# First layer: gate products strip by strip; third layer: q and k copies inside the softplus

## What is computed

```python
# first layer
o_attn = swa_sink_attention(q, k, v, sinks[i])      # 8 heads, softmax with a sink
...
y = jnp.einsum('blgn,gpn->blgp', h_re, c_re) - jnp.einsum('blgn,gpn->blgp', h_im, c_im)
y = y.reshape(b, l, SSM_WIDTH) + d_skip.astype(f32) * uf
y = jax.nn.gelu(y)
out = y * jax.nn.sigmoid(y @ w_glu.astype(f32) + b_glu.astype(f32))
...
mixed = jnp.concatenate([o_attn, o_ssm], axis=-1) @ even_w_out[i]

# stick-breaking attention, 16 heads
z = jnp.einsum('bhqd,bhkd->bhqk', q_blk, kt).astype(jnp.float32) * scale
log_keep = jnp.where(mask, jax.nn.log_sigmoid(-z), 0.0)
log_survive = lax.cumsum(log_keep, axis=3, reverse=True) - log_keep
weights = jnp.where(mask, jnp.exp(jax.nn.log_sigmoid(z) + log_survive), 0.0)
return jnp.einsum('bhqk,bhkd->bhqd', weights.astype(vt.dtype), vt)
```

## Time and profile before

| | us |
|---|---|
| median of 3 runs | 1596.52 |
| lowest, highest | 1591.95, 1599.69 |
| the profiled execution | 1599.0 |
| its span, first to last instruction | 1597.2 |
| PE busy | 1547.9 (97%) |
| DVE, ACT, POOL busy | 1193.1, 863.6, 262.8 |
| mean granted clock of PE | 0.988 of 2.4 GHz |

### The profile page before, as it was taken

How to read it: one execution, slowest core, us unless ns; L and a number is a source line. 1 busy time by engine, 2 the same in 40 slices (tenths; PEclk the granted TensorE clock), 3 DMA queues, 4 the chain that set the end, 5 groups by cost and what they waited for, 6 DMA issues and landing times.

```text
span 1597.2 us, 30962 instructions
## 1 busy us (share of the span) xinstructions
PE 1547.9 (97%) x10555; PEld 1365.1 (85%) x10555; DVE 1193.1 (75%) x2322; ACT 863.6 (54%) x1323; POOL 262.8 (16%) x110
## 2 busy tenths in 40 slices
PE   7889999999999999999999999999999999999998
PEld 7877888888878887898899999988888888878887
DVE  6987888725778887666599853399999999975555
ACT  6755444458754444746456566555554444445543
POOL 2001000155110001100377856600000000000000
PEclk9899999999999999999999999999999999999999
DMA  6125665543466565433545556555555555555564
GB/s 217 62 80 161 195 192 187 184 146 106 137 195 196 186 194 182 130 100 106 172 159 172 171 177 192 185 171 170 171 171 169 172 171 173 174 178 189 192 196 145
DMA packets 72557, 264.67 MB, mean 166 GB/s; under 512 B 8080, under 2 KB 8336, under 8 KB 72112
## 3 DMA queue, kind: packets, MB, share of 16 engines
q1 hardware_dynamic: 71744, 261.00, 50.6%
q10 hardware_dynamic: 752, 2.83, 0.5%
HBM read 262.75 MB, written 1.05 MB: 165 GB/s over the span
## 4 chain that ended last, share of the span: by engine, by line
PE 87%; DVE 4%; ACT 2%; issue 1%; ACTq 0%; DVEq 0%
PE ps L550 17%; PE ps L639 11%; PE ps L640 11%; PE ps L651 10%; PE ps L554 9%; PE ps L538 6%; PE ps L542 6%; PE ps L539 6%; PE ps L1086 2%; PE ps L584 1%; PE ps L592 1%; PE ps L586 1%; DVE arena L1690 1%; DVE hT L1728 1%; DVE w_lo L1690 1%
## 5 line engine op out<-in xcount | busy, mean ns | idle before, releaser
L1177 ACT ACTIVATE w_hi<-ring 128x1024 fp32r<-128x1024 f32 x489 | 515.7, 1057 | 334.0 <-PE ps L651 206.3
L1690 DVE TENSOR_TENSOR w_lo<-ring,w_hi 128x1024 fp32r<-128x1024 f32 x388 | 473.0, 1220 | 97.7 <-ACT w_hi L1177 83.6
L2537 POOL TENSOR_TENSOR w_lo<-ring,w_hi 128x1024 fp32r<-128x1024 f32 x101 | 254.1, 2528 | 759.8 <-DVE w_lo L1690 378.8
L550 PE MATMUL ps<-hT,w_hi 128*128 128x512 f32 x1216 | 308.8, 395 | 3.3 <-DVE hT L1728 2.6
L639 PE MATMUL ps<-w_hi,halves_hi 128*128 128x512 f32 x688 | 271.5, 395 | 2.5 <-DVE w_lo L1690 2.0
L640 PE MATMUL ps<-w_hi,halves_lo 128*128 128x512 f32 x688 | 268.7, 391 | 0.0
L550 PEld LDWEIGHTS ps<-hT,w_hi 128*128 128x128 f32 x1216 | 220.7, 189 | 47.5 <-issue 3.0
L538 PE MATMUL ps<-hT,w_hi 128*128 128x256 f32 x984 | 250.5, 291 | 5.7 <-DVE hT L1728 3.9
L539 PE MATMUL ps<-hT,w_hi 128*128 128x256 f32 x984 | 246.5, 287 | 0.0
L538 PEld LDWEIGHTS ps<-hT,w_hi 128*128 128x128 f32 x984 | 192.3, 195 | 10.3 <-issue 7.6
L539 PEld LDWEIGHTS ps<-hT,w_hi 128*128 128x128 f32 x984 | 192.6, 196 | 0.0
(11 more groups left out here) (301 smaller groups left out, 1590.5 us busy)
## 6 DMA issues: line engine op xcount, KB each, us to landing
ring<-in_strips SPq DMA_DIRECT2D x489, 512.0 KB, 3.5
const<-in_const SPq DMA_DIRECT2D x1, 1352.0 KB, 11.8
x_s<-in_x SPq DMA_DIRECT2D x2, 512.0 KB, 4.6
arena<-in_rel ACTq DMA_DIRECT2D x1, 1024.0 KB, 5.6
arena<-in_keys ACTq DMA_DIRECT2D x1, 1024.0 KB, 7.2
out<-x_s SPq DMA_DIRECT2D x4, 256.0 KB, 2.3
arena<-in_ssm_bc SPq DMA_DIRECT2D x1, 512.0 KB, 6.9
arena<-in_ssm_b SPq DMA_DIRECT2D x1, 512.0 KB, 8.1
```

Source lines behind the costliest of these rows:

```text
L550: pe.matmul(bank, w[0][:, c * P:(c + 1) * P], hT[:, c].rearrange("p s t -> p (s t)"), start=c == 0, stop=False, skip_group_check=True)
L1177: sc.activation(w_hi[:, n % RING, :], ring[:, n % RING, :], ACT.Copy).then_inc(high_ready, 1)
L1690: return ve.tensor_tensor(o, a, b, op)
L2537: po.tensor_tensor(w_lo[:, n % RING, :], ring[:, n % RING, :], w_hi[:, n % RING, :].bitcast(F32), ALU.subtract).then_inc(low_ready, 1)
```

## The change

Four edits. (1) PE computes all products of gate strip 0, then all of strip 1, and no longer waits for the low half of strip 1 before the first. (2) DVE takes `y(3)` directly behind `y(2)`, ahead of the low half of gate strip 1, and the rest of y(1) behind both; ACT makes the high half of `out` strip 4 ahead of gelu(2) instead of gelu(3). (3) DVE's two `scale_of` calls stand behind the first reduction, and behind the scans of ssm(0). (4) In the third stage the copies of q and k of pairs 1 and 2 are made inside the softplus of the pair before.

```diff
                 def glu(cs):
-                    w = [split(AT[("even", "glu", n)]) for n in range(2)]
-                    low_halves(w[1])
-                    for c in cs:
-                        pe.wait_ge(y_low, c + 1)
-                        for n in range(2):
+                    for n in range(2):
+                        w = split(AT[("even", "glu", n)])
+                        low_halves(w)
+                        for c in cs:
+                            pe.wait_ge(y_low, c + 1)
                             for j in range(2):
...
-                            if c == 3:
-                                mm.then_inc(strip_done, 1)
+                        mm.then_inc(strip_done, 1)
...
                     if j == 2:
-                        high_to(AT[("even", "glu", 1)])
-                    if j == 3:
                         high_to(AT[("even", "out", 4)])
...
-                    if g:
-                        scale_of(0)
                     ve.wait_ge(score_out, 4 * g + 4)
...
                         ch.add(ve.tensor_reduce(two(0)[:, part, :], e_S[g][:, :, lo:hi], AX, ALU.max))
+                        if g and part == 0:
+                            scale_of(0)
...
                     if j == 0:
-                        scale_of(1)
                         ve.wait_ge(decay_rows, 1)
                         ve.wait_ge(zeroed, 5)
                     ch.add(ve.tensor_tensor_scan(z[:, 0, :], m, z[:, 0, :], 0.0, ALU.mult, ALU.add))
                     ch.link(ve.tensor_tensor_scan(z[:, 1, :], m, z[:, 1, :], 0.0, ALU.mult, ALU.add))
+                    if j == 0:
+                        scale_of(1)
...
                 ssm(3)
+                low(AT[("even", "glu", 0)])
                 y(2)
+                y(3)
                 y_rest(1)
-                low(AT[("even", "glu", 0)])
                 low(AT[("even", "glu", 1)])
-                y(3)
                 y_rest(2)
                 y_rest(3)
...
-                def project(j):
+                def project(j, parts=range(2)):
...
                     ve.scalar_tensor_tensor(out=sp, in0=bank_pair(j), scalar=0.0, in1=o_t, op0=ALU.max,
                                             op1=ALU.add).then_inc(sp_ready, 1)
+                    if j < 2:
+                        project(j + 1, [1 - j])
...
                     ve.tensor_copy(o_sp_hi, sp).then_inc(sp_high, 1)
+                    if j == 1:
+                        project(2, [1])
...
                 for j in range(8):
-                    project(j)
+                    if j == 0:
+                        project(0)
+                        project(1, [0])
+                    if j > 2:
+                        project(j)
```

More of the change, by code:

```diff
@@ L766, in glu @@
                 def glu(cs):
-                    w = [split(AT[("even", "glu", n)]) for n in range(2)]
-                    low_halves(w[1])
-                    for c in cs:
-                        pe.wait_ge(y_low, c + 1)
-                        for n in range(2):
+                    for n in range(2):
[3 more added lines that the diff above has]
+                            pe.wait_ge(y_low, c + 1)
                             for j in range(2):
                                 cols = slice(c * T + j * P, c * T + (j + 1) * P)
-                                mm = mm3(ps[:, 6 + n, j * T:(j + 1) * T], w[n][0][:, cols], w[n][1][:, cols],
+                                mm = mm3(ps[:, 6 + n, j * T:(j + 1) * T], w[0][:, cols], w[1][:, cols],
                                          hT_hi[:, c, :], hT_lo[:, c, :], c == 0 and j == 0, c == 3,
                                          skip_group_check=True)
-                            if c == 3:
-                                mm.then_inc(strip_done, 1)
+                        mm.then_inc(strip_done, 1)
                 def probs_turned(ns):
@@ L2094, in diagonal @@
                     return a.rearrange("p h (b c) -> p h b c", c=P)[:, :, 0:3:2, :]
-                def project(j):
+                def project(j, parts=range(2)):
                     if j == 0:
                         ve.wait_ge(evac, FIRST)
-                    for n, (name, dst) in enumerate((("q", o_qT), ("k", o_kT))):
+                    for n in parts:
+                        name, dst = (("q", o_qT), ("k", o_kT))[n]
                         m = FIRST + 2 * j + n
```

## The result

The changed kernel took 1587.73 us (median of four; 1586.53 to 1591.35) against 1597.34 us for the kernel before (median of four, three of them those of the table before): a ratio of 0.9947, 95% interval 0.9921 to 0.9973, 8.5 us less (the two medians are 9.6 us apart). The forecast was 1592.6 us with a range from 1587.5 us: the time lies 0.2 us inside its fast end, and outside the forecast's own range of 1590 to 1596 us. A gain of over 0.5% was given a chance of 0.10.

What follows compares the result with a forecast made beforehand. TensorE, busy 97% of the span, was taken as the bound, so only its waits or lower clock could be won. Gate 2.2 us plus third layer 1.7 us made 3.9 us: 1592.6 us, own range 1590 to 1596, wider range 1587.5 to 1597.5.

Steps and rivals of the forecast that it cites:

- The gate: First layer: gate products strip by strip start `out` strip 4 2.3 us sooner; 2.2 us booked, bounds 1.2 to 2.9.
- the 0.1 us taken off for it: First layer: gate gain of 2.3 us booked as 2.2, since the high half of `out` strip 5 might come late.
- The reciprocals: First layer: first state about 1.2 us sooner, but nothing booked, since later values wait for ACT's normalising.
- The first pair shifts by at most 0.1 us: First layer: moving the first reciprocals behind a DVE reduction, issued about when ACT is done, delays them at most 0.1 us.
- the sum: Whole kernel: 2.2 us at the gate plus 1.7 us in the third layer, 3.9 us, giving 1592.6 us against the median.
- The softplus: Third layer: earlier q and k copies win 3.3 us, less 1.6 us for DVE meeting POOL: 1.7 us, bounds -0.7 to 3.3.
- I take the clock to stay up: Third layer, pair 1: full clock kept behind the new pauses of 0.6 and 1.3 us; 1.5 of 2.7 us won is clock.
- DVE ahead of GpSimd: Rival, third layer: DVE's low part gets in before POOL, or the cost is hidden; gain 5.5 us, 1591.0 us, chance 0.20.
- The clock falls at the new pauses: Rival, gate or pair 1: 3.4 us at the lower clock cost 1.7 us; 1594.3 us, chance 0.13.
- Gate's gain met by the next wait: Rival: `out` strip 5 waits instead, little left in the third layer; 0.5 us in all, 1596 us, chance 0.10.
- GpSimd's meeting in pairs 2 to 7: Rival, third layer: the DVE-POOL meeting recurs, six pairs pay 1.6 us each; 5.7 us slower, 1602.2 us, chance 0.05.

Runs made afterwards that it cites:

- the changed kernel taken again: The kernel with all four edits, run once more without any further edit, against the kernel before: 1587.59 us (6 runs), ratio 0.9948.
- the control: The kernel before, unchanged, run once more as if it were a changed one: 1597.36 us (12 runs), ratio 0.9997.
- the first series: First batch of runs: gate, reciprocals and softplus edits each alone, and all edits again, beside the kernel before (28 runs, mean clock 0.9900).

## Why the prediction was right or wrong

**The gate: right.** Forecast 2.2 us (the times gave 2.3), measured 2.44 to 2.46 us in all nine profiles with the edit. `out` strip 4 starts behind the last gate product with no wait, and strip 5 without one too: its high half was not late, so the 0.1 us taken off for it was not needed. PE had one wait (0.49 us) where two were expected.

**The reciprocals: right that the work gives nothing, wrong that the edit gives nothing.** The 1.3 us sooner at the states (forecast 1.2) and their return at ScalarE's normalising came as told. Two steps were wrong. "The first pair shifts by at most 0.1 us" holds for a late ScalarE only, as in the profile before. Where it comes early, it waits 1.98 us for the reciprocal, and 1.26 us where that stands first, and PE pays those 0.7 us ahead of the first scores. And the sum had no term for the clock: a first state that is earlier divides PE's pause otherwise, and the fall near 80 us, which every profile without the edit has, is missing in seven of eight. The net of the two is small, about 0.4 us by the traces.

**The softplus: right in its chain, by its own steps.** In the changed kernel taken again, z(1) comes 2.6 us sooner on the lead (forecast 2.6), PE waits 1.34 us ahead of cum(0) (1.3), GpSimd starts 0.48 us ahead of DVE's low part (0.4), that part takes 2.69 us (over 2), PE waits 1.45 us (1.6), and the third layer gives 1.85 us (1.7). The Trainium skill ("SBUF — State Buffer", on the two separate sides of SBUF) has the port pair as an exclusive lock for a whole instruction. The run in which GpSimd waits agrees: 0.95 us for the same operation when GpSimd is not running. The rule's other side shows too: GpSimd's two low halves took 5.43 us beside DVE's operation and 4.76 us without.

In the first profile after, the step "I take the clock to stay up" failed: it fell at 356.1 us, behind a wait of 1.35 us. DVE's copy of k then came late (364.89 us), met GpSimd's run later (1.47 us for the low part, PE's wait 0.23 us), and the third layer still gave 1.54 us. A fall and a meeting do not add up: whichever comes first hides the other.

**The rivals.** DVE ahead of GpSimd: in no profile without GpSimd's wait. The clock falls at the new pauses: in three of eight profiles in the third layer, and never at the gate; its sign was the wrong one, since it was priced as a loss, against a kernel before that I took to lose 1.5 us there once. That kernel loses more in four profiles of five. A fall of 3.4 us was priced at 1.7 us and cost 1.2 to 1.5. Gate's gain met by the next wait: no. GpSimd's meeting in pairs 2 to 7: no; the lead stands at 5.2 to 5.3 us from 375 to 417 us.

**The step that failed** is that the sum treated the granted clock of one trace as a property of the kernel before, to be kept everywhere but at z(1). What the forecast lacked is a term for the falls that removed pauses remove: about 0.4 us from 70 to 87 us (1.1 us with both reciprocals moved against 0.7 without, the 0.7 us at the first scores paid), 0.7 us at the gate (1.49 in two profiles of four), and 0.5 us more in the third layer (four profiles of five, 0.56 to 0.77 us each). With the 2.45 us of the gate and the 1.75 us of the third layer (mean of the change's three profiles) these make 5.8 of the 8.3 us.

**What stays open** is the rest, 2.5 us. At least 1.5 us of it appear between 632 and 722 us, where no edit lies and PE's waits are the same (1.8, 0.6 and 0.9 us in each). All seven profiles with both the gate and the softplus edit gain there (1.5 us in four, 3.1 us in three); the six that lack one or both gain nothing (-0.15 to 0.02 us). The clock is down for 6.8 us there or for 3.4 us, against 10.2 us. The seven arrive there 6.4 to 9.3 us ahead of the profile before, the six at most 4.1 us, but among the seven the gain does not follow the lead (3.1 us at a lead of 6.4, 1.5 us at one of 7.9), and no run tells why.

## What to carry to other kernels

A pause of TensorE costs its own length and, some of the time, a stretch at 1.2 GHz behind it. In this kernel the edits that shorten or split pauses were worth about twice as much together as at equal clock (8.3 against 4.1 us), part of it in places far from the edits; give the clock a term of its own, with both signs. Read the granted clock from more than one execution before building on it, and compare kernels at equal clock, or with each other's mean clock beside the times. An operation of VectorE with both operands in SBUF that is moved to just behind the start of a GpSimd run pays the rest of GpSimd's instruction (the copy out of PSUM inside the same run kept its 0.42 us), and one wait on GpSimd, where its result is not due, takes that away in the trace (1.5 us of TensorE); the runs here were too few to show it in the time.

## What the runs showed of the hardware

- The same kernel with the same waits is at 1.2 GHz behind one pause in one execution and not in the next: behind the gate's wait of 1.9 us it was at 1.00 in the profile before and 0.60 in the control. The same holds for 1.35 us of waiting in the third layer (down in three profiles, not in five).
- The mean clock of single runs went from 0.989 to 0.994 in the kernel before and from 0.989 to 0.997 with the reciprocals alone. Of the 28 runs of before in the first series the slowest (1599.51 us) had 0.989 and the fastest (1592.15 us) 0.993: at 0.93 us for each 0.001, this is 3.7 of their 7.4 us.
- VectorE's low part took 0.96, 1.47 or 2.69 us by when it came in GpSimd's run, and GpSimd's own pair of instructions 4.76, 5.73 or 5.43 us.
